# A hybrid RWKV and Fourier layer on one core: the scan's operands made inside the projection stage, in place of a stage of their own

## The reference, cut to what matters

```python
u = h @ w_in                                          # h: (1152 tokens, 1024), w_in: 35 tiles of 128 columns
rkv = short_conv(u[..., :OFF_WD], conv_rkv)           # 3 taps; r, k, v: 512 channels each
wd, ad, gd, f = ...                                   # next columns of u
gates = sigmoid(u[..., OFF_GATE:] + gate_b)
w_log = -softplus(-(w0 + tanh(wd) @ w_up)) - 0.5      # per direction (forward, backward)
decay = exp(-exp(w_log))
a = sigmoid(a0 + ad @ a_up)                           # per direction
kk = k * k_k;  kk = kk / max(sqrt(sum(kk * kk)), 1e-12)      # per head of 64
k_dir = k * (1 + (a - 1) * k_a)
# scan over tokens, per direction: S = S * w - (S kk) (kk * a)^T + v k^T;  o = S r
```

## Time and profile before

| what | value |
|---|---|
| median of 3 runs | 3337.89 us (3336.18 to 3338.34) |
| the profiled execution | 3336.4 us |
| its span | 3334.6 us |
| TensorE matmuls busy | 2971.5 us (89%) |
| VectorE, ScalarE, GpSimd busy | 1478.8, 779.7, 335.0 us |
| transfers | 270.56 MB, 81 GB/s in the mean |

### The profile page before, as it was taken

How to read it: one execution, slowest core, us unless ns; L and a number is a source line. 1 busy time by engine, 2 the same in 40 slices (tenths; PEclk the granted TensorE clock), 3 DMA queues, 4 the chain that set the end, 5 groups by cost and what they waited for, 6 DMA issues and landing times. The chain is left out here.

```text
span 3334.6 us, 56908 instructions
## 1 busy us (share of the span) xinstructions
PE 2971.5 (89%) x23416; PEld 2794.6 (84%) x23416; DVE 1478.8 (44%) x2519; ACT 779.7 (23%) x1300; POOL 335.0 (10%) x298
## 2 busy tenths in 40 slices
PE   5799999999997999983199996969979999999998
PEld 2499999999986999982188883769969999999996
DVE  0443334333345411416688857235563343434334
ACT  1321111111113222326133333321241111111112
POOL 0300000000003000006411213012240000000000
PEclk7899999999998999996599997989999999999999
DMA  9311111111111222326643412242101111111111
GB/s 407 137 39 38 39 58 47 44 38 38 38 57 61 81 94 100 123 93 245 208 110 89 103 22 105 76 153 81 50 32 56 52 38 44 38 38 38 38 38 63
DMA packets 175226, 270.56 MB, mean 81 GB/s; under 512 B 69104, under 2 KB 124400, under 8 KB 170480
## 3 DMA queue, kind: packets, MB, share of 16 engines
q1 hardware_dynamic: 175088, 268.60, 23.5%
HBM read 211.07 MB, written 57.48 MB: 81 GB/s over the span
## 5 line engine op out<-in xcount | busy, mean ns | idle before, releaser
L474 DVE SCALAR_TENSOR_TENSOR x<-bank,gate,x 128x128 f32<-128x128 f32 (+1 forms) x832 | 411.5, 516 | 209.7 <-PE bank L573 209.2
L609 DVE TENSOR_TENSOR g_ffn<-act_out_ffn,bank 128x384 f32<-128x384 f32 x132 | 73.2, 554 | 743.1 <-ACT act_out_ffn L606 743.1
L558 PE MATMUL bank<-h_hi_ffn,wlo_a_ffn 128*128 128x384 f32 x1056 | 357.0, 338 | 21.1 <-DVE h_lo_ffn L325 11.3
L606 ACT ACTIVATE act_out_ffn<-bank 128x384 f32<-128x384 f32 x132 | 65.0, 492 | 1247.1 <-PE bank L558 1247.1
L558 PE MATMUL bank<-h_lo_ffn,whi_a_ffn 128*128 128x384 f32 x1056 | 355.9, 337 | 0.0
L558 PE MATMUL bank<-h_hi_ffn,whi_a_ffn 128*128 128x384 f32 x1056 | 355.6, 337 | 0.0
L573 PE MATMUL bank<-g_hi_ffn,wlo_d_ffn 128*128 128x384 f32 x1056 | 352.9, 334 | 2.4 <-DVE g_lo_ffn L494 2.4
L573 PE MATMUL bank<-g_hi_ffn,whi_d_ffn 128*128 128x384 f32 x1056 | 352.7, 334 | 0.0
L558 PE MATMUL bank<-h_hi_ffn,whi_b_ffn 128*128 128x384 f32 x1056 | 352.7, 334 | 0.0
L573 PE MATMUL bank<-g_lo_ffn,whi_d_ffn 128*128 128x384 f32 x1056 | 352.7, 334 | 0.0
L558 PE MATMUL bank<-h_hi_ffn,wlo_b_ffn 128*128 128x384 f32 x1056 | 352.7, 334 | 0.0
(11 more groups left out here) (230 smaller groups left out, 4955.6 us busy)
## 6 DMA issues: line engine op xcount, KB each, us to landing
ada_raw<-in_ada_w SPq DMA_DIRECT2D x36, 1024.0 KB, 11.3
raw_a_ffn<-in_ffn_w SPq DMA_DIRECT2D x44, 512.0 KB, 4.5
raw_b_ffn<-in_ffn_w SPq DMA_DIRECT2D x44, 512.0 KB, 4.4
raw_d_ffn<-in_ffn_w SPq DMA_DIRECT2D x44, 512.0 KB, 3.2
streams<-wo_outs SPq DMA_DIRECT2D x32, 576.0 KB, 3.0
raw_in<-in_w_in SPq DMA_DIRECT2D x35, 512.0 KB, 3.9
mix<-row_out SPq DMA_DIRECT2D x23, 576.0 KB, 3.0
sc_ar<-streams SPq DMA_DIRECT2D x36, 256.0 KB, 3.3
```

Of the source, the lines that this page charges most:

```text
L474: ins = nc.vector.scalar_tensor_tensor(xs, kit.banks[4 + d % 4][:, a:b], kit.gate[:, gate, d, cond:cond + 1], xs, ALU.mult, ALU.add)
L558: mm = nc.tensor.matmul(kit.banks[2 * slot + j][:, 0:CH], w[q][:, par, cols], v[:, k, toks], start=(k == 0 and m == 0), stop=(k == ku - 1 ...
L606: return self.nc.scalar.activation(out, a, ACT.Silu)
L609: self.nc.vector.tensor_tensor(g32, act_out, b, ALU.mult).then_inc(g32_ready, 1)
```

## The change

The stage `wide_operands` and the class `UnitKeys` are gone. `projection` now works through 35 positions p in a written-out order: low-rank tiles first (p = 0, 1), then v (2 to 5), k (6 to 9), r (10 to 13), the gate row (14), Fourier rows (15 to 18), gates (19 to 34). From p = 10 on, every channel tile ct of the scan's operands has a window of six positions, w = 0 to 5: low-rank products of the backward direction beside w0 and of the forward one beside w1 (`lora_up`, into banks 6 and 7 alone), the next channel tile's key sums beside w2 and w3, the exponentials (`powers`) at w3, the operands (`products`) at w4 and w5. The rows are worked on in place: rates become running sums and then inverse decays; learn and keep become operands; k, r and keys lie in the space of x, which is saved. The kernel's `sp.dma_start` calls of the window stand in the one queue with the w_in rows. One operand of the backward direction is stored from `g_pad`, whose rows have 65 columns, so it goes in 2304 pieces of 64 floats. GpSimd turns v and does kk * a, k_dir and their sum, reading backward where the direction asks for it.

```diff
-class UnitKeys:
...
-def projection(kit, mix, x_saved, keys, cst):
...
-def wide_operands(kit, cst, mix, keys, kd_sum, streams, v_back, g_last):
...
+def projection(kit, mix, x_saved, cst, kd_sum, streams, v_back, g_last):
...
+    ORDER = [J_WD, J_AD] + list(range(8, 12)) + list(range(4, 8)) + list(range(0, 4)) + list(range(J_GD, J_END))
+    CONV_AT, V_AT, WT, W_AT = 2, 2, 6, 10
+    part = lambda c: slice(c * CH, (c + 1) * CH)
+    by_chunk = lambda v: v.rearrange("p (k t) -> p k t", t=CK)
+    conv_index = lambda p: p - CONV_AT if CONV_AT <= p < CONV_AT + 12 else None
+    window = lambda p: divmod(p - W_AT, WT) if W_AT <= p < W_AT + WT * CT else (None, None)
...
+        rates, learn, keep = (buf("wo_" + n, [P, 2, T]) for n in ("rates", "learn", "keep"))
+        g_pad = buf("wo_g_pad", [P, 2, T // CK, CK + 1])
+        a_out = buf("wo_a_out", [P, T])
+        k_row, r_row, kk = kit.x[:, 0], kit.x[:, 1], kit.x[:, 2:4]
+        sq, v_turned = a_out[:], kit.x[:, 0:2]
+        reset = kd_sum[:, CT - 1]
+
+
+        outs = lambda d: tuple(by_chunk(v) for v in (a_out[:], r_row, learn[:, d], keep[:, d]))\
+            if d == 0 else (by_chunk(padded[:, 0, 0:T]), g_pad[:, 1, :, 1:CK + 1], by_chunk(learn[:, 1]), by_chunk(keep[:, 1]))
...
+            def store_operands(ct, d):
+                for q, out in enumerate(outs(d)):
+                    sp.wait_ge(S["out_ready"], outs_before(ct, d) + q + 1)
+                    sp.dma_start(by_chunk(streams[d, q, ct]), out).then_inc(stored[d], 16)
...
+            for p in range(J_END):
+                j, par = ORDER[p], p % 2
+                if p + 1 < J_END:
+                    sp.wait_ge(w_ready, p + 1)
+                    sp.dma_start(raw[:], kit.dram["w_in"][ORDER[p + 1]]).then_inc(loaded, 16)
+                if conv_index(p) is not None:
+                    sp.wait_ge(conv_done, conv_index(p) + 1)
+                    sp.dma_start(mix[j][:, 0:T_CTX], row[:, par, 1:T_CTX + 1]).then_inc(row_stored[par], 16)
+                    sp.dma_start(mix[j][:, T_CTX:T], row[:, par, T_CTX + 3:T + 3]).then_inc(row_stored[par], 16)
...
+                    sp.wait_ge(evicted, p * 3 + 3)
+                    sp.dma_start(mix[j], row[:, par, 0:T]).then_inc(row_stored[par], 16)
+                if V_AT < p <= V_AT + CT:
+                    ct = p - 1 - V_AT
+                    sp.wait_ge(S["v_turned"], ct + 1)
+                    sp.dma_start(v_back[ct], v_turned[:, ct % 2]).then_inc(v_stored[ct % 2], 16)
+                if p == 3:
+                    rows_stored(2)
+                    for m in range(2):
+                        for d in range(2):
+                            sp.dma_start(lora[LORA * m:LORA * (m + 1), d], mix[J_WD + m][LORA * d:LORA * (d + 1)])\
+                                .then_inc(S["lora_in"], 16)
+                if p == 7:
+                    sp.wait_ge(saved, 16 * KT)
+                    sp.dma_start(reset, kit.dram["reset"]).then_inc(S["reset_in"], 16)
+                    rows_stored(7)
+                    load_keys(0)
+                ct, w = window(p + 1)
+                if w == 0:
+                    if ct == 0:
+                        rows_stored(9)
+                        sp.wait_ge(v_stored[0], 32)
+                    else:
+                        rows_stored(10)
+                        sp.wait_ge(S["kd_ready"], 2 * ct)
+                    sp.dma_start(k_row, mix[CT + ct]).then_inc(S["k_in"], 16)
+                    if ct + 1 < CT:
+                        load_keys(ct + 1)
+                if w == 3:
+                    if ct:
+                        rows_stored(14)
+                        sp.wait_ge(stored[0], 64 * ct)
+                    else:
+                        rows_stored(11)
+                        sp.wait_ge(v_stored[1], 32)
+                    sp.dma_start(r_row, mix[ct]).then_inc(S["r_in"], 16)
+                ct, w = window(p)
+                if w == 4:
+                    store_operands(ct, 1)
+                if w == 5:
+                    store_operands(ct, 0)
...
+            def learning(ct, d, c):
+
+                n = 6 * ct + (0 if d else 3) + c
+                if c == 0 and ct:
+                    act.wait_ge(S["out_ready"], outs_before(ct - 1, d) + 4)
+                    act.wait_ge(stored[d], 64 * ct)
+                for m, (dst, name, ready) in enumerate(((rates[:, d], "w0", "lam_ready"), (learn[:, d], "a0", "a_ready"))):
+                    act.wait_ge(S["lora_done"], 2 * n + m + 1)
+                    src, bias = bank[6 + m], kit.col(name, d * CT + ct)
...
+                        top = T + T_CTX - 1 - c * CH
+                        ins = nc.scalar.activation(dst[:, top:top - CH:-1], src[:, 0:CH], ACT.Sigmoid, bias=bias)
+                    ins.then_inc(S[ready], 1)
...
+            def powers(ct, d):
+                i = 2 * ct + 1 - d
+                act.wait_ge(S["cum_ready"], i + 1)
+                act.wait_ge(S["pads"], 2)
+                nc.scalar.activation(g_pad[:, d, :, 1:CK + 1], by_chunk(rates[:, d]), ACT.Exp, scale=-DECAY_SCALE)
+                nc.scalar.activation(g_last[:, d, ct], by_chunk(rates[:, d])[:, :, CK - 1], ACT.Exp, scale=-DECAY_SCALE)\
+                    .then_inc(S["g_ready"], 1)
+                act.wait_ge(S["g_ready"], i + 1)
+                nc.scalar.activation(rates[:, d], rates[:, d], ACT.Exp, scale=DECAY_SCALE).then_inc(S["ig_ready"], 1)
...
+            for p in range(J_END):
+                j, par = ORDER[p], p % 2
...
+                    act.wait_ge(proj_done, p * 3 + c + 1)
+                    src = bank[3 * par + c]
...
+                    if c == 0 and p + 1 < J_END:
+                        high(p + 1)
+                    if (p, c) == (W_AT - 2, 0):
+                        square(0)
+                    if (p, c) == (W_AT - 1, 1):
+                        root(0, 0)
+                        root(0, 1)
+                    if (p, c) == (W_AT - 1, 2):
+                        root(0, 2)
+                    ct, w = window(p)
+                    if w is None:
+                        continue
+                    if w == 0:
+                        learning(ct, 1, c)
+                    if w == 1:
+                        learning(ct, 0, c)
+                        if c == 0:
+                            kept(ct, 1)
+                        if c == 2 and ct + 1 < CT:
+                            square(ct + 1)
+                    if w == 2:
+                        if c == 0:
+                            kept(ct, 0)
+                        if c == 2 and ct + 1 < CT:
+                            root(ct + 1, 0)
+                            root(ct + 1, 1)
+                    if w == 3 and c == 1:
+                        if ct + 1 < CT:
+                            root(ct + 1, 2)
+                        powers(ct, 1)
+                        powers(ct, 0)
...
+            def products(ct, d):
+                i = 2 * ct + 1 - d
+                a, r, b, k = outs(d)
+                if ct:
+                    dve.wait_ge(stored[d], 64 * ct)
+                if ct + 1 < CT:
+                    dve.wait_ge(S["kk_ready"], NC * (ct + 2))
+                dve.wait_ge(S["g_ready"], i + 1)
+                for at, to, v in met(d, kk[:, ct % 2]):
+                    ins = nc.vector.tensor_tensor(a[:, at // CK:to // CK], by_chunk(v),
+                                                  g_pad[:, d, at // CK:to // CK, 0:CK], ALU.mult)
+                ins.then_inc(S["out_ready"], 1)
...
+            for d in range(2):
+                nc.vector.memset(g_pad[:, d, :, 0:1], 1.0).then_inc(S["pads"], 1)
+            for p in range(J_END):
+                if p + 1 < J_END:
+                    low(p + 1)
+                if p == W_AT - 2:
+                    scale(0)
+                if conv_index(p) is not None:
+                    convolve(p)
+                if p == W_AT - 1:
+                    divide(0)
+                ct, w = window(p)
+                if w == 0 and ct + 1 < CT:
+                    scale(ct + 1)
+                if w == 1:
+                    add_up(ct, 1)
+                if w == 2:
+                    add_up(ct, 0)
+                if w == 3 and ct + 1 < CT:
+                    divide(ct + 1)
+                if w == 4:
+                    products(ct, 1)
+                if w == 5:
+                    products(ct, 0)
...
+            def lora_up(ct, d, c):
+                n = 6 * ct + (0 if d else 3) + c
+                if n == 0:
+                    pe.wait_ge(const_loaded, 32)
+                    pe.wait_ge(S["lora_in"], 64)
+                if n % 6 == 0:
+                    pe.wait_ge(S["kk_rooted"], NC * (ct + 1))
+                for m, ready in enumerate(("lam_ready", "a_ready")):
+                    pe.wait_ge(S[ready], n)
+                    rows = slice(LORA * m, LORA * (m + 1))
+                    nc.tensor.matmul(bank[6 + m][:, 0:CH], lora_w[rows, d, ct * P:(ct + 1) * P], lora[rows, d, part(c)],
```

(86 more changed lines are left out.)

471 lines of the change are left out of this document (153 added, 318 removed).

## The result

The changed kernel takes 3377.39 us (median of 4 runs, 3374.16 to 3379.65), the kernel before beside it 3338.11: ratio 1.0115, interval 1.0103 to 1.0128, so 34 to 43 us slower. The forecast was slower by 12, at 3350, so the direction was right and the size was off by 27. The forecast's own range (3335 to 3362) missed the time; the wider one that was to hold 8 in 10 (3305 to 3378) held it by less than 1 us. The profiled execution took 3376.26, its span 3374.5.

A forecast was written before the change was run, and what follows sets the result against it. The prediction took the projection as bound by TensorE, the operand stage by VectorE, GpSimd and ScalarE in turn. Stops of 118.5 plus 30.7 of products, less 137.1 removed, gave net +12.1 us: 3350 us, range 3335 to 3362.

The forecast's parts named there:

- what goes: Operand stage behind the projection, 132.0 us, and four stops in the key sums, 5.1 us, disappear: 137.1 us removed.
- w0's second pair: At w0's second third TensorE stops while ScalarE rounds a late w_in row before the sigmoids: 49.8 us, cold clock included.
- early tiles: Tiles p = 3 to 9: transfers ahead of the w_in row, and a late key sum at p = 9, stop TensorE 11.9 us.
- twelve plain stops: Thirds of w0 and w1 where low-rank products wait for ScalarE to draw the pair before: 1.5 us each, 18.0 together.
- w1's second pair: At w1's middle third ScalarE's rounding also precedes the low-rank products: 2.4 us three times, 3.8 at p = 11, sum 11.0.
- the squares: At w2 ScalarE's square of the next keys stands ahead of the key sums: 3.0 us three times, 9.0.
- w5 and the next windows: Eviction behind powers delays w5's row, four stores the next window's, plus 1.0 per small-piece store, three times: 6.5 us.
- rival A: Queued transfers share the 16 engines, so the w_in row gets through early: 3296 us if always, 3323 if half; chance 0.32.
- the clock: TensorE's slower clock after long idling costs 1.9 us; stops of 1.27 leave the pitch at 0.17 to 0.19.
- rival B: More cold clock: each TensorE stop of 2 to 5 us also costs 1.9, some 13 stops, +25, 3375 us; chance 0.12.
- VectorE's order at p = 13: Late eviction, then convolution and divide(1) ahead of tile 15's subtraction on VectorE: TensorE stops 10.4 plus 1.9 of clock, 12.3 us.
- the small pieces: One d = 1 store from g_pad in 256-byte pieces takes 1.3 to 3.7 us against 1.4; +1.0 taken, three times.

## Why the prediction was off, step by step

**Right: what goes.** 132.6 us of stage for 132.0; 5.1 of key-sum stops.

**Right: the products.** 1.30 us per pair, 31.2 for 24, against 30.7.

**Right: the idle time, in sum and in most parts.** Idle after, against the forecast's waits without clock: w0's second pair 42.6 (41.1); early tiles 14.3 (11.9; 5.6, 0.9, 5.4 and 2.5); twelve plain stops 13.1 idle and 3.5 of refilling (18.0); w1's second pair 10.8 (11.0); the squares 7.8 (9.0); the start of p = 14 and 15 9.6 (10.4); w5 and the next windows 7.2 (6.5). With 1.2 before the first pair of all (the 1.1 for the roots), 106.6. Inside the early tiles the parts differ more than their sum: at p = 9 the stop is 5.4 where 2.6 was forecast, because the first key sums also wait for the scaling on VectorE and the square on ScalarE, both behind the late row's subtraction; and of three stops of 0.7 only one came, of 0.9. The feed does not cover itself (rival A): the row was there 10.1 us after its issue at ct = 1, 15.4 into its tile, where the in-order sum said 14.4 to 15.0.

**The step that failed: the clock.** "Stops of 1.27 leave the pitch at 0.17 to 0.19; nothing lies between 1.27 and 8", and of the two ends I took nothing for the stops in between, keeping 9.5 us for five long ones (one of the five, at p = 15, came out at 5.99 and is among the 13 in between). The runs put it on the other side. The clock is mis-sized by some 16 us (26 measured, 9.5 forecast), refilling by 5 (10, against 4 to 5 in the plain stops), the idle time by 2: 23 to 24 of the 27. The rest is within the scatter of one execution. That is rival B, given 0.12 and 3375 for a time of 3377. With the two ends at 1.27 (nothing) and 9.87 (1.9), a stop of 4 to 6 us is not plainly nearer to the first, and I priced all of them by it.

**Right by chance: VectorE's order at p = 13.** 10.4 was forecast as one stop and came as the sum of two. Only the second (5.99) ends with VectorE's order, and moving the subtraction took 2.9 of it; the first (3.62) is the row of p = 14, behind a convolution that GpSimd had slowed from 3.7 to 6.9 us. The prediction had GpSimd's products in w1 and w2 at nothing. And the order could not be mended alone, because SyncE's queue handed the delay on.

**Right: the small pieces.** 1.3 more per store for the 1.0 taken. The rule of the Trainium skill ("DMA: Bandwidth & Descriptors", the table at its head), by which I would have gone to 3.7 us, has the direction right: below 512 bytes the rate falls, here from 403 to 213 GB/s, and the store takes 2.8. How much of the fall comes from the small pieces and how much from their odd offsets is not shown.

**What the gain turned into.** The change removes 138 us and pays 31 for products. Almost none of the rest is work: 107 are waits and 35 what waits bring with them. The experiments give most of it back by order alone (3264 against 3377), with the same arithmetic.

## What to carry to other kernels

When work moves beside a stage that TensorE fills, first walk the feed of that stage: what stands between a row's store and the next load in SyncE's queue, and what ScalarE does between the load and the first thing that TensorE needs. Price every stop of more than 3 us with its refilling and a cold stretch (0.3 plus some 1.3 to 2.7 us here, and 0.9 more where a pair of small products comes first), one of 2 to 3 us with about half of that, and break up stops of 1 us by placing the small products inside a block of large ones. Issue the next weight row ahead of all transfers that nobody waits for soon; here the subtraction could then be moved without the stop turning up one tile later (1.11 in place of 10.22).

## What the runs showed of the hardware

TensorE's clock fell to the lower level (granted 0.50, 1.2 GHz, pitch 0.32 against 0.17) behind every stop of 3.6 to 12 us in the changed kernel, behind some of 2.1 to 2.7 and not behind others of the same length, and behind none of 1.0 to 1.3. The other ten profiles blur the short end: over all eleven, a cold stretch followed 4 of 157 stops of 0.9 to 1.3 us and 42 of 77 of 2.0 to 3.3. What tells two stops of one length apart stays open.

When VectorE and GpSimd work at the same time, the one that starts second takes longer: beside GpSimd a convolution of 3.7 us took 6.9 and a subtraction of 1.23 took 2.79; beside VectorE's running sum, which kept its usual 2.55, GpSimd's product of 2.7 took 4.9.

A store in 256-byte pieces, taken from rows of 65 floats, moved 213 GB/s where whole rows moved 403.
